# Four pairs of weight tiles with the contraction outermost, the squared norm taken after the second product in three quarters, one tensor at an aligned place in SBUF, and one transfer issued later

## The reference

```python
def first_block(x, ...):
    ...
    merged = g_a * (y_pool @ w_proj_pool) + g_b * (y_nsa @ w_proj_nsa)
    x = x + merged @ w_out
    h = rms_norm(x, norm_mlp)
    x = x + jnp.square(jax.nn.relu(h @ w_ff1)) @ w_ff2      # d_ff = 4096
    return rms_norm(x, norm_final)

def second_block(x, c, ...):
    shift1, scale1, gate1, shift2, scale2, gate2 = split(silu(c) @ ada_w + ada_b, 6)
    h = rmsnorm(x, norm1_g) * (1.0 + scale1) + shift1
    qa, ka, va, fa, qb, kb, vb, ga, gb = split(h @ w_in)
    ...                                                      # two attentions, merged
    x = x + gate1 * (merged @ w_out)
    h2 = rmsnorm(x, norm2_g) * (1.0 + scale2) + shift2
    y = hierarchical_moe(h2, ...)     # top group, top 2 of its 4 experts; d_ff of an expert 512
    x = x + gate2 * y
    return rmsnorm(x, final_g)
```

## Time and profile before

| | |
|---|---|
| median of 3 runs | 1695.74 us (1693.26 to 1696.0) |
| profiled execution, span | 1701.1 us, 1699.3 us |
| TensorE, busy | 1573.1 us (93%) |
| VectorE | 858.0 us (50%) |
| ScalarE | 742.9 us (44%) |
| GpSimd | 669.4 us (39%) |
| mean of the 16 DMA engines | 163 GB/s, 276.16 MB moved |

### The profile page before, as it was taken

One profiled execution on the slowest core, in us unless ns is written; L12 is line 12 of the kernel. 1 busy time (PEld: TensorE's weight loads), 2 busy tenths in 40 slices (PEclk: granted clock), 3 DMA queues, 4 the chain that ended last, 5 costly groups with the idle time before them and its releaser, 6 DMA issues.

```text
span 1699.3 us, 19539 instructions
## 1 busy us (share of the span) xinstructions
PE 1573.1 (93%) x7315; PEld 1212.2 (71%) x7315; DVE 858.0 (50%) x1441; ACT 742.9 (44%) x1186; POOL 669.4 (39%) x421
## 2 busy tenths in 40 slices
PE   7987899999999998998997999999999699999983
PEld 6664565888877777877785777777877477777772
DVE  5348886143134536364325233431012589999994
ACT  5215786223243323132343443632232377777772
POOL 3235564444564544444452563644454100000003
PEclk9989999999999999999996999999999799999996
DMA  6410000322234666576420331212235489999944
GB/s 242 143 62 25 1 1 28 128 87 96 91 112 136 238 219 225 198 246 235 140 99 25 124 112 44 69 63 76 98 106 209 186 323 390 392 388 397 390 192 165
DMA packets 78685, 276.16 MB, mean 163 GB/s; under 512 B 9525, under 2 KB 10853, under 8 KB 78585
## 3 DMA queue, kind: packets, MB, share of 16 engines
q1 hardware_dynamic: 69712, 245.89, 40.7%
q10 hardware_dynamic: 6568, 20.57, 3.2%
q0 software_dynamic: 2304, 8.39, 1.3%
HBM read 244.37 MB, written 30.45 MB: 162 GB/s over the span
## 4 chain that ended last, share of the span: by engine, by line
PE 72%; DVE 12%; ACT 5%; DMA 4%; issue 3%; POOL 3%; SPq 0%; PEldq 0%; ACTq 0%; DVEq 0%; POOLq 0%
PE ps L416 16%; PE ps L420 15%; PE ps L417 15%; PE ps L878 3%; PE ps L874 2%; PE ps L875 2%; DMA RAW<-in_w_ff 2%; DVE RS L292 2%; DVE TMP L1390 2%; PE ps L892 2%; PE ps L893 2%; PE ps L896 2%; PE ps L713 1%; PE ps L624 1%; ACT RS L287 1%
## 5 line engine op out<-in xcount | busy, mean ns | idle before, releaser
L292 POOL TENSOR_TENSOR RS<-RAW,RS 128x1024 fp32r<-128x1024 f32 x174 | 423.7, 2436 | 501.6 <-ACT RS L287 501.5
L287 ACT ACTIVATE RS<-RAW 128x1024 fp32r<-128x1024 f32 x306 | 318.8, 1056 | 289.6 <-DMA RAW<-in_w_ff 124.0
L416 PE MATMUL ps<-RH,RS 128*128 128x512 f32 x928 | 376.9, 406 | 32.6 <-POOL RH L2189 14.2
L420 PE MATMUL ps<-RH,RS 128*128 128x512 f32 x928 | 368.9, 397 | 0.9 <-POOL RS L292 0.9
L417 PE MATMUL ps<-RH,RS 128*128 128x512 f32 x928 | 368.9, 398 | 0.0
L416 PEld LDWEIGHTS ps<-RH,RS 128*128 128x128 f32 x928 | 178.7, 193 | 83.2 <-POOL RH L2189 16.6
L420 PEld LDWEIGHTS ps<-RH,RS 128*128 128x128 f32 x928 | 178.6, 192 | 41.1 <-POOL RS L292 1.7
L417 PEld LDWEIGHTS ps<-RH,RS 128*128 128x128 f32 x928 | 179.1, 193 | 37.9 <-issue 1.7
L420 PE MATMUL ps<-RA,RS 128*128 128x512 f32 x416 | 166.0, 399 | 0.0
L292 DVE TENSOR_TENSOR RS<-RAW,RS 128x1024 fp32r<-128x1024 f32 x132 | 154.0, 1222 | 22.2 <-ACT RS L287 21.7
L416 PE MATMUL ps<-RA,RS 128*128 128x512 f32 x416 | 164.9, 396 | 0.0
(11 more groups left out here) (344 smaller groups left out, 2368.4 us busy)
## 6 DMA issues: line engine op xcount, KB each, us to landing
RAW<-in_w_ff SPq DMA_DIRECT2D x64, 512.0 KB, 4.9
RAW<-in_w_gate SPq DMA_DIRECT2D x46, 512.0 KB, 6.3
RAW<-in_w_up SPq DMA_DIRECT2D x45, 512.0 KB, 7.0
RAW<-in_w_down SPq DMA_DIRECT2D x39, 512.0 KB, 6.1
PB<-in_ada SPq DMA_DIRECT2D x24, 512.0 KB, 4.1
TB<-in_ada SPq DMA_DIRECT2D x24, 512.0 KB, 3.8
xs<-TB SPq DMA_DIRECT2D x23, 512.0 KB, 6.5
M<-in_w_down SPq DMA_DIRECT2D x17, 512.0 KB, 6.0
```

The lines of the kernel that those rows point to most:

```text
L287: act.activation(RS[:, spl[n], 0, :], raws[slot[n]], ACT.Copy).then_inc(*HI.up(n))
L292: eng.tensor_tensor(RS[:, s, 1, :], raws[slot[n]], hif(RS[:, s, 0, :]), ALU.subtract).then_inc(*mark.up(n))
L416: pe.matmul(b[:, :], wh, xh, start=(k == 0), stop=False)
L420: last = pe.matmul(b[:, :], wl, xh, start=False, stop=(k == K - 1))
```

## The change

1. RA and RAW2 are declared directly behind RH. By the declarations RA now begins at byte 65,536 of a partition, and all tensors behind it lie 32,768 bytes further.
2. A new helper `dense_two` takes two weight units together, with k outermost: for each k it waits once for the input block and issues three matmuls for either unit, into two banks. It is used for w_out 0 and 1, for w_ff1 0 and 1 of the first quarter, for w2_fa 0 with w2_qa 0, and for w2_out 0 and 1. In the first quarter the row sums of the norm, formerly between w_ff1 0 and 1, come behind both.
3. In quarters 0 to 2 the multiplication by the squared norm factor leaves the w_ff1 steps (24 DVE operations) and is done on the result of w_ff2: `scaled_residual` multiplies the bank by RST into TMP and adds TMP to X, two DVE operations where there was one. The last quarter keeps the old order. Squaring RST moves from step x = 0 to x = 1.
4. In the mixture of experts `load_x(1)` goes from ahead of the first gate units' splits to behind the first up units' splits.

The diff, without the declarations' move (RA and RAW2 from the end of the list to behind RH):

```diff
@@ -423,6 +423,26 @@
                 else:
                     last.then_inc(*P.up(key))
 
+        def dense_two(units, R, ready, banks=ALL8):
+
+            tiles_ = [IDX[u] for u in units]
+            bs = [take(u, banks) for u in units]
+            for k in range(8):
+                pe.wait_ge(*ready(k))
+                for key, n, b in zip(units, tiles_, bs):
+                    s, c = spl[n], 128 * k
+                    wh, wl = RS[:, s, 0, c:c + 128], RS[:, s, 1, c:c + 128]
+                    xh, xl = R[:, 0, k, :], R[:, 1, k, :]
+                    if k == 0:
+                        pe.wait_ge(*HI(n))
+                    pe.matmul(b[:, :], wh, xh, start=(k == 0), stop=False)
+                    pe.matmul(b[:, :], wh, xl, start=False, stop=False)
+                    if k == 0:
+                        pe.wait_ge(*lo(n))
+                    last = pe.matmul(b[:, :], wl, xh, start=False, stop=(k == 7))
+                    if k == 7:
+                        last.then_inc(*P.up(key, ("fed", n)))
+
         def dense_rows(name, R, banks, ready=None):
 
             for u in range(4):
@@ -660,8 +680,9 @@
             dense("w_ga", m, RH, 0, 8)
             if m % 2 == 1:
                 dense("w_pp", m // 2, RA, 0, 4, (lambda k: V(("ya", k))) if m == 1 else None)
-        for m in range(8):
-            dense("w_out", m, RH, 0, 8, (lambda k: V(("mg", k)) if k % 2 == 0 else G(("mg", k))) if m == 0 else None)
+        dense_two([("w_out", 0), ("w_out", 1)], RH, lambda k: V(("mg", k)) if k % 2 == 0 else G(("mg", k)))
+        for m in range(2, 8):
+            dense("w_out", m, RH, 0, 8)
 
 
         def modulation(J):
@@ -676,7 +697,10 @@
 
         for f in range(4):
             for m in range(8):
-                dense("w_ff1", 8 * f + m, RA, 0, 8, (lambda k: V(("ha", k))) if f == m == 0 else None, RB)
+                if f == m == 0:
+                    dense_two([("w_ff1", 0), ("w_ff1", 1)], RA, lambda k: V(("ha", k)), RB)
+                elif f or m > 1:
+                    dense("w_ff1", 8 * f + m, RA, 0, 8, None, RB)
                 if f == m == 0:
                     pe.wait_ge(*V(("sq2", 7)))
                     row_sums(("rms", 2), RST, RB)
@@ -751,8 +775,8 @@
             for u in us:
                 dense(name, u, RH, 0, 8, None, RB)
 
-        dense("w2_fa", 0, RH, 0, 8, lambda k: V(("h2", k)), RB)
-        projected("w2_qa", 0, 1, 2, 3)
+        dense_two([("w2_fa", 0), ("w2_qa", 0)], RH, lambda k: V(("h2", k)), RB)
+        projected("w2_qa", 1, 2, 3)
         projected("w2_ka", 0, 1)
         pair_scores(0)
         projected("w2_ka", 2)
@@ -803,8 +827,9 @@
             dense("w2_gb", m, RH, 0, 8, None, RB)
             dense("w2_gb", m + 1, RH, 0, 8, None, RB)
             dense("w2_sb", m // 2, RA, 4, 4, (lambda k: V(("ev", ("po", 4 + k)))) if m == 0 else None, RB)
-        for m in range(8):
-            dense("w2_out", m, RH, 0, 8, (lambda k: V(("mg2", k)) if k % 2 == 0 else G(("mg2", k))) if m == 0 else None)
+        dense_two([("w2_out", 0), ("w2_out", 1)], RH, lambda k: V(("mg2", k)) if k % 2 == 0 else G(("mg2", k)))
+        for m in range(2, 8):
+            dense("w2_out", m, RH, 0, 8)
 
 
         pe.wait_ge(*V(("sq5", 7)))
@@ -1341,8 +1366,6 @@
                 load_x(u0)
                 load_x(u0 + 1)
             prep(u0)
-            if not u0:
-                load_x(1)
             for u in range(u0, u1):
                 tiles("w_gate", u)
                 if u >= 2:
@@ -1352,6 +1375,7 @@
                     prep(u + 1)
                 tiles("w_up", u)
                 if u == 0:
+                    load_x(1)
                     prep(1)
                 if u + 2 < u1:
                     load_x(u + 2)
@@ -1706,6 +1730,16 @@
             dve.wait_ge(*P((name, u)))
             tt(X[:, m, :], X[:, m, :], ps[name, u], ALU.add, ("ev", (name, u)))
 
+        def scaled_residual(name, u, m):
+
+            j = 2 + m % 2
+            dve.wait_ge(*P((name, u)))
+            if u == 0:
+                after("rst2")
+            tt(TMP[:, j, :], ps[name, u], RST, ALU.mult, ("ev", (name, u)))
+            after(("ev", (name, u)))
+            tt(X[:, m, :], X[:, m, :], TMP[:, j, :], ALU.add, ("x1", u))
+
         def last_square(tag, prev):
             dve.wait_ge(*A((tag + "a", 7)))
             dve.wait_ge(*prev)
@@ -1753,14 +1787,18 @@
                     row_root(("rms", 2))
                     after(("rr", ("rms", 2)))
                     diagonal(("rmsb", 2), 0, 3)
+                elif x == 1:
                     dve.wait_ge(*A(("ev", ("rmsb", 2))))
                     tt(RST, RST, RST, ALU.mult, "rst2")
                 dve.wait_ge(*A(("relu", x)))
                 if x >= 2:
                     dve.wait_ge(*(G(("ft", x - 2)) if i else A(("fh", x - 2))))
-                tt(TMP[:, 2 + i, :], TMP[:, i, :], ps["w_ff1", x], ALU.mult, ("ev", ("w_ff1", x)))
-                after(("ev", ("w_ff1", x)))
-                tt(TMP[:, 2 + i, :], TMP[:, 2 + i, :], RST, ALU.mult, ("ff", x))
+                if f < 3:
+                    tt(TMP[:, 2 + i, :], TMP[:, i, :], ps["w_ff1", x], ALU.mult, ("ev", ("w_ff1", x)), ("ff", x))
+                else:
+                    tt(TMP[:, 2 + i, :], TMP[:, i, :], ps["w_ff1", x], ALU.mult, ("ev", ("w_ff1", x)))
+                    after(("ev", ("w_ff1", x)))
+                    tt(TMP[:, 2 + i, :], TMP[:, 2 + i, :], RST, ALU.mult, ("ff", x))
                 if i == 0:
                     dve.wait_ge(*A(("fh", x)))
                     tt(RH[:, 1, m, :], TMP[:, 2, :], hif(RH[:, 0, m, :]), ALU.subtract, ("ft", x))
@@ -1784,7 +1822,10 @@
                 tt(gsc[:, 16:24], gsc[:, 0:8], vecs[:, VG_FIN:VG_FIN + 8], ALU.mult, "ggs")
             for m in range(8):
                 splits_dve(dve, IDX["w_ff2", 8 * f + m])
-                residual("w_ff2", 8 * f + m, m)
+                if f == 3:
+                    residual("w_ff2", 24 + m, m)
+                else:
+                    scaled_residual("w_ff2", 8 * f + m, m)
                 if f == 3 and m == 7:
                     last_square("sq3", G(("sq3", 6)))
                 if f == 3 and m:
```

More of the change, by code:

```diff
@@ L173, in build_program @@
     RH = sb("RH", [128, 2, 8, S], F32R)
+    with nc.sbuf_tensor("RA", [128, 2, 8, S], F32R) as RA:
+        pass
+    RAW2 = sb("RAW2", [128, 8, 1024])
     RAW = sb("RAW", [128, NRAW, 1024])
@@ L203, in build_program @@
     EXI = sb("EXI", [1, 8], I32)
-    with nc.sbuf_tensor("RA", [128, 2, 8, S], F32R) as RA:
-        pass
-    RAW2 = sb("RAW2", [128, 8, 1024])
     ps = Psum([ctx.enter_context(nc.psum_tensor(f"ps{i}", [128, 512], F32))[:, :] for i in range(8)])
```

## The result

The changed kernel takes 1670.01 us (median of 4 runs, 1667.88 to 1672.48) against 1694.58 for the kernel before in the same comparison: ratio 0.9834, 95% interval 0.981 to 0.9858 (the two medians alone give 0.9855). By the medians that is 24.6 us faster; 1660 was predicted, with 1648 to 1676 as range. The profiled execution took 1668.56 us (span 1666.6), 32.5 less than the profiled one before; 35.8 was the sum of the prediction.

A forecast was written before the change was run, and what follows sets the result against it. TensorE, busy 93% of the span, was taken as the bound. Terms 8.3+12.5+5.5+4.5+5.0+0 = 35.8 us bring the profiled execution to 1665.3 and the median to 1660; range 1648 to 1676, the forecast's own 1653 to 1667.

The forecast's parts named there:

- rival B: Load loop stays late, quarters gain 4 instead of 12.5 us, pair in quarter 0 adds lateness: 1669 to 1672; chance 0.12.
- RA's place: RA's 1248 matmuls each 6.7 ns quicker if the start address is the reason: 8.3 us.
- Rival A: RA's slower step has another cause than its address: 1668; chance 0.08.
- The quarters: Multiplication moved behind w_ff2 shrinks TensorE's gaps at three changes from w_ff1 to w_ff2: 12.5 us, bounds 4 and 16.8.
- The pair at w_ff1: Quarter 0's w_ff1 0 and 1 together: removes no gap there, makes unit 0's bank 5.4 us later.
- w_out and w2_out: Pairing units 0 and 1 removes pauses and slow clock: 5.5 and 4.5 us, lower bounds 2.9 and 2.2.
- w2_fa: Pairing w2_fa with w2_qa, where VectorE supplies one k every 2.20 us: 5.0 us gained, bounds 2 and 7.5.
- the rule named with it: At w2_fa, going on without pauses raises the clock early: pair ends near 931.6, 7.4 us gained instead of 5.0.
- The expert's load: load_x(1) later in the mixture of experts: 0, bounds 9.5 us gained and 4 lost.
- Rival C: Scatter isn't slowed by the loads and the expert's rows come early: up to 9.5 us more, 1650; chance 0.10.
- Rival D: w_ff2 steps become bound by VectorE, 69 us if all reaches the path: 1729; chance 0.04.
- From the profiled execution to the median: The 5.4 us by which the earlier profiled execution exceeded the median of three runs, taken off at the end.

The follow-up runs named there:

- e1: The changed kernel with padding so that RA starts 32 bytes past a multiple of 64: 1674.02 us.
- e8: The changed kernel with SyncE issuing each MLP weight's load ahead of the ada weight's that stood before it: 1653.78 us.
- e12: The changed kernel with the ada unit of each w_ff1 step but the very first ahead of VectorE's wait for the relu: 1652.53 us.
- e3: The changed kernel with w_ff1 0 and 1 of the first quarter one after the other again: 1668.43 us.
- e4: The changed kernel with load_x(1) back ahead of the first gate units' splits: 1672.55 us.
- e13: The changed kernel with ada units ahead of the relu's wait and weight loads from w_gate (2, 2) on held until expert 1's rows landed: 1643.05 us.
- e9: The changed kernel with weight loads from w_up (2, 0) on held until expert 1's rows have landed: 1667.54 us.

## Why the prediction was right or wrong

The time fell inside the range and on the predicted side, 10 us above the predicted value. It lies outside the forecast's own range, 1653 to 1667, and inside the 1669 to 1672 of rival B. By its own steps:

- **RA's place**, 8.3: right. The step went to 0.2267, and e1 brought 0.2333 back by 32 bytes. The 8.3 remains the step times the count. Rival A has fallen.
- **The quarters**, 12.5: the step that failed. The removed multiplication was 1.80 of the 12.59 of the earlier trace rows, and the prediction let the loop shrink by that, to 10.79, with every other term as it was. It became 11.5. When the multiplication went, the ada unit behind it moved forward into the time of POOL's low part and took 2.48 instead of 1.29, and the load took 6.44 instead of 5.49; that the rounding and the square left the chain as well gave back less than these two took. The add in w_ff2 steps behaved the same way, at no cost: below are VectorE's groups after, and X<-X,TMP takes 0.865 on average.

```profile
L1414 DVE TENSOR_TENSOR TMP<-ps,RT 128x512 f32<-128x512 f32 x42 | 28.9, 690 | 113.6 <-PE ps L420 113.6
L1778 DVE SCALAR_TENSOR_TENSOR M<-TB,small,M 128x1024 f32<-128x1024 f32 x16 | 24.0, 1500 | 0.0
L1414 DVE TENSOR_TENSOR X<-X,TMP 128x512 f32<-128x512 f32 x24 | 20.8, 865 | 0.8
```

  Stretches 0 to 2 won 7.8 together, of which RA's step is 30 x 24 x 6.7 ns = 4.8, so 3.0 remain for the move and the pair's lateness. That is below the prediction's lower bound of 4, and this was the quickest of the four executions: the others (316.2 to 318.7) win 0.9 to 3.5 less than RA's share alone, so that nothing is left for the move with its pair. The bound itself was added up wrongly, since three times 1.8 to 2.2 is 5.4 to 6.6. This is rival B, whose 4 in place of 12.5 was the nearer figure: the loop through ada unit, SyncE and load kept its lag. e8 and e12 show it, since each opens the loop at another point and each wins 15 us in the stretches. What the ada unit's 2.48 by itself costs was not shown: in e8 and e12 these units stay long or grow longer, and the gaps are gone.
- **The pair at w_ff1** was given no gain at its own place and a lateness of 5.4. The lateness is shown by e3 (8.1 with the clock's share), and it made the first gap 5.46 where 2.5 was predicted. The gain at its place, 2.0 besides RA's step, was not seen: the clock stays at 1.00 over the norm's spread.
- **w_out and w2_out**, 5.5 and 4.5: 5.6 and 4.5.
- **w2_fa**, 5.0: 7.6. A little outside the bounds of 2 and 7.5. Here the rule named with it was the better forecast. Without pauses at half clock the clock rose inside the pair (mean 0.88), and from the fourth k on TensorE waited for VectorE again, 0.16 to 0.55 us for each, at full clock. The page meant is the Trainium skill's "TensorE: Matmul & The Clock Gate", HAM oscillation; the 7.4 worked out beside it was within 0.2 of what was measured. In e1 the clock was at 1.00 before the pair began, and the pair took the same 16.7: with six matmuls for each k, VectorE's 2.20 us for one is what sets its length. The prediction's 934.3, from which it had 4.7, does not follow from its rows: a pair done at 935.1 and a clock that rises at 936 make 3.5.
- **The expert's load**, 0: cost 1.9 in the profiled pair, about 2 by e4, within chance. The mechanism was as described, with the wait at the transposes. The scatter's last piece went from 7.55 to 14.49 us; e13 and e4 show that the weight loads beside it did that, and e9 that they lengthen the fetch. The clock loss of about 2.1 in the bound of 9.5 is not that of the second MLP gap, which the prediction itself has as 2.55. The Trainium skill's rule ("DMA: Bandwidth & Descriptors", Issuing engines are not separate DMA queues) holds in this case; by it the term would have been a loss. Rival C has fallen.
- **Rival D** has fallen: w_ff2 steps stay TensorE's own (in e12 the eight w_ff2 units of quarter 1 take 43.5 us, 5.44 each).
- **From the profiled execution to the median**: 5.4 us were taken off for good, but they were chance. The stage from the start to w_out takes 460.2 to 466.2 us in executions of kernels whose work is the same up to there (in one with RA's slower step), and stretch 0 took 129.6 to 134.6 in five with the pair and the loop as changed. The profiled execution before was 6.5 above its median, the one after 1.5 below. The terms as measured are 8.3+3.0+2.0+5.6+4.5+7.6-1.9 = 29.1; the other 3.4 of the 32.5 between the profiled executions lie in stages that the change does not touch. So of the 10 us some 7 are the sum's error (35.8 against 29.1) and the rest is chance that was carried through a single profiled execution.

## What to carry to other kernels

When an operation is taken out of a loop, work out the loop again with the operations behind it at their new places, and price each by what runs beside it there. An in-order list (here the loads of SyncE) ties two streams together; look for the stream with slack that stands ahead of the one without, and exchange them before shortening anything. Where an engine's input arrives slowly, give it a second consumer of the same input: the three pairs at such places gave 17.6 us, and the clock came with them. The fourth, at w_ff1, where no input was late, won 2 and cost 8 downstream until the loop was opened. And compare stages between numbered instructions rather than medians: effects of 2 us showed there under a scatter of 5, in stages that do not hang on the loop of the loads; those that do differ by 5 us from one execution to the next.

## What the runs showed of the hardware

- A matmul of 128x512 float32 whose moving operand starts 32 bytes past a multiple of 64 has a step of 0.2333 us; at a multiple of 64 it is 0.2267 (kernel before, e1, changed kernel).
- The ada unit on VectorE, with two SBUF inputs, took 1.27 us alone, 2.46 when it began in the midst of an operation of GpSimd, and 3.50 when the two began together; when it began first it took 1.28, and GpSimd's operation behind it 3.15 instead of 2.4. Operations of 128x512 with one input in PSUM took 0.68 to 0.69 on average in each of their groups. The Trainium skill ("SBUF — State Buffer", Who interferes with whom) describes this as a port held by one of the two at a time, and these rows agree. The two rows of the changed kernel show the ada unit beginning in the midst of GpSimd's operation, those of the kernel before show it beginning first:

```profile
541.43 2.43 POOL L292 TENSOR_TENSOR RS<-RAW,RS 128x1024 fp32r<-128x1024 f32 x1 [1.59 <-ACT RS L287]
542.47 2.46 DVE L1778 SCALAR_TENSOR_TENSOR M<-TB,small,M 128x1024 f32<-128x1024 f32 x1
```

```profile
560.49 1.28 DVE L1744 SCALAR_TENSOR_TENSOR M<-PB,small,M 128x1024 f32<-128x1024 f32 x1
560.88 3.15 POOL L292 TENSOR_TENSOR RS<-RAW,RS 128x1024 fp32r<-128x1024 f32 x1 [2.25 <-ACT RS L287]
```

- The last piece of the scatter took 4.8 to 7.6 us with no load of 512 KB from another queue issued beside it (e4, e13, before), and 10.0 to 14.5 with eight beside it (seven executions).
